# Feeding one expert tile instead of two by choosing products, and requesting gate rows and third down weights later

## What is computed

```python
g_w, g_idx = lax.top_k(g_prob, 1)
...
e_val, e_idx = lax.top_k(e_in, TOP_K)          # two experts of the chosen group
e_w = jax.nn.softmax(e_val, axis=-1) * g_w
...
hid = jax.nn.silu(jnp.einsum('nd,edf->nef', xt, w_gate)) * jnp.einsum('nd,edf->nef', xt, w_up)
hid = hid * combine[:, :, None].astype(hid.dtype)
out = jnp.einsum('nef,efd->nd', hid, w_down)
```

## Time and profile before

| | us |
|---|---|
| median of three runs | 1282.0 |
| lowest, highest | 1281.82, 1284.33 |
| the profiled execution's own time | 1282.83 |
| its span | 1281.0 |
| TensorE busy in the span | 1212.7 (95%) |
| VectorE, ScalarE, POOL busy | 590.9, 441.2, 58.0 |
| share of TensorE in the chain that ended last | 74% |
| share of DMA in that chain | 7% |
| mean granted TensorE clock | 0.991 |

### The profile page before, as it was taken

How to read it: one execution, slowest core, us unless ns; L and a number is a source line. 1 busy time by engine, 2 the same in 40 slices (tenths; PEclk the granted TensorE clock), 3 DMA queues, 4 the chain that set the end, 5 groups by cost and what they waited for, 6 DMA issues and landing times.

```text
span 1281.0 us, 16366 instructions
## 1 busy us (share of the span) xinstructions
PE 1212.7 (95%) x5099; PEld 653.0 (51%) x5100; DVE 590.9 (46%) x1348; ACT 441.2 (34%) x903; POOL 58.0 (5%) x63
## 2 busy tenths in 40 slices
PE   6999999999999999999969998899999999999997
PEld 4555555555554474443325444566654574444443
DVE  1332555555543664222328545887834653222216
ACT  2433656565641121110112326677722111111122
POOL 0103000000000120000021000000000210000002
PEclk9999999999999999999989999899999999999999
DMA  9979999632363177999975001500020369989947
GB/s 370 413 304 376 395 414 413 259 103 103 125 244 144 48 280 232 353 356 360 372 284 224 9 1 50 218 1 2 1 99 1 115 264 331 354 291 333 355 183 266
DMA packets 88641, 289.68 MB, mean 226 GB/s; under 512 B 9369, under 2 KB 27740, under 8 KB 87292
## 3 DMA queue, kind: packets, MB, share of 16 engines
q1 hardware_dynamic: 46176, 185.23, 39.6%
q0 software_dynamic: 16640, 64.59, 13.0%
q10 hardware_dynamic: 25756, 38.98, 9.0%
HBM read 214.03 MB, written 74.73 MB: 225 GB/s over the span
## 4 chain that ended last, share of the span: by engine, by line
PE 74%; DMA 7%; ACT 6%; DVE 5%; SPq 3%; issue 3%; ACTq 1%; DVEq 1%; POOL 0%; POOLq 0%
PE ps L2208 15%; PE ps L1785 11%; PE ps L1804 11%; PE ps L1727 7%; PE ps L2237 6%; PE ps L2088 4%; DMA arena<-in_moe_gu 4%; PE ps L1909 3%; PE ps L2287 3%; PE ps L2051 3%; PE ps L1838 2%; PE ps L2150 2%; ACT arena L746 2%; PE ps L2061 2%; PE ps L1747 2%
## 5 line engine op out<-in xcount | busy, mean ns | idle before, releaser
L2208 PE MATMUL ps<-arena 128*128 (+1 forms) x560 | 246.3, 593 | 0.0
L1727 PE MATMUL ps<-const,arena 128*128 128x128 f32 (+2 forms) x1000 | 145.0, 278 | 24.8 <-DMA const<-in_const 8.1
L2208 PEld LDWEIGHTS ps<-arena 128*128 128x128 f32 x560 | 103.8, 190 | 117.3 <-issue 117.2
L1727 PEld LDWEIGHTS ps<-const,arena 128*128 128x128 f32 (+2 forms) x1000 | 114.8, 142 | 84.9 <-issue 44.5
L1785 PE MATMUL ps<-arena 128*128 128x512 f32 (+2 forms) x400 | 152.1, 535 | 4.8 <-DVE arena L1306 1.4
L1187 DVE TENSOR_REDUCE hst<-ps 128x1 f32<-128x640 f32 (+1 forms) x160 | 111.0, 715 | 85.7 <-PE ps L2088 71.1
L1804 PE MATMUL ps<-arena 128*128 128x512 f32 x320 | 142.0, 597 | 1.4 <-issue 1.4
L2237 PE MATMUL ps<-arena 128*128 (+1 forms) x280 | 126.1, 593 | 2.2 <-ACT arena L890 2.2
L746 ACT ACTIVATE arena<-ps,hst 128x640 f32<-128x640 f32 (+1 forms) x160 | 112.6, 707 | 40.2 <-DVE hst L1187 39.9
L1785 PEld LDWEIGHTS ps<-arena 128*128 128x128 f32 x400 | 74.4, 190 | 74.3 <-issue 58.6
L1804 PEld LDWEIGHTS ps<-arena 128*128 128x128 f32 x320 | 59.1, 190 | 69.8 <-issue 69.7
(11 more groups left out here) (233 smaller groups left out, 1199.7 us busy)
## 6 DMA issues: line engine op xcount, KB each, us to landing
arena<-in_moe_gu SPq DMA_DIRECT2D x128, 512.0 KB, 12.7
arena<-in_ada_w SPq DMA_DIRECT2D x62, 768.0 KB, 11.9
slot_rows<-arena POOLq DMA_DIRECT2D x10, 4096.0 KB, 68.3
arena<-in_moe_w_down SPq DMA_DIRECT2D x64, 512.0 KB, 15.5
slot_rows<-arena ACTq DMA_DIRECT2D x33, 512.0 KB, 9.6
arena<-slot_rows ACTq DMA_DIRECT2D x124, 128.0 KB, 13.6
arena<-mod_rows SPq DMA_DIRECT2D x12, 512.0 KB, 13.2
arena<-in_gqa_w_qkv SPq DMA_DIRECT2D x12, 512.0 KB, 13.7
```

The costliest lines, as they stand in the source:

```text
L1727: return nc.tensor.transpose(out, in_, ident[0:rows, 0:rows])
L2208: last = mm(bank(gu_bank(u)), e_xsT[:, nth(u, D)][:, k * P:(k + 1) * P], w(k * BANK, BANK), start=k == 0, stop=k == KD - 1)
```

## The change

`FED` becomes 1: only tile 0 is made by choosing products, with 128 moving columns instead of 256, in banks 4 and 5. Tile 1 is read back like tile 2, right before it, and transposed on VectorE. What used to hang on the same number but does not change (POOL's list of landings, the counts in the plan) gets a constant of its own, `HELD` = 2. One comparison replaces two in `choose_first`; since tile 0 holds expert 0, it looks at the lower of a token's two row numbers (`R_LOW`), which `place_rows` now keeps. VectorE starts the plan before the copy of the fed tile and no longer has `hid` of tile 0 in its middle; the sums of pair weights move to the end of the layer. TensorE's order for the first two tiles becomes gate/up 0, turn 0, down 0, gate/up 1. SP requests the third down weights after tile 2's rows have landed, and the gate rows and the fetch of modulation vectors in the loop over experts, at expert 4.

```diff
--- before.py
+++ after.py
@@ -113,6 +113,7 @@
...
 GATHERS_EARLY = 3
+GATES_AT = 4
 
@@ -122,7 +123,7 @@
...
 C_R4 = C_CQ + TOK
-FED, FIXED = 2, 3
+FED, HELD, FIXED = 1, 2, 3
 PIECE = 1024
@@ -178,7 +179,8 @@
...
 R_PL = R_BEF + NTILE * NE
-R_FREE = R_PL + 2 * NTILE
+R_LOW = R_PL + 2 * NTILE
+R_FREE = R_LOW + NTILE
 RWC = 32
@@ -562,12 +564,8 @@
...
             load_dn(l, 1)
+            sp.wait_ge(S("xs_landed2", l), 16 * XQ)
             load_dn(l, 2)
-            if l == 0:
-                mod_fetch(1, 1)
-            sp.wait_ge(S("h_ready"), NTILE * (l + 1))
-            for v in range(2):
-                sp.dma_start(gate_m[:, v * D:(v + 1) * D], modrow[l][v, 5:6, :].broadcast_to([P, D])).then_inc(S("gates_m"), 16)
             sp.wait_ge(S("routed"), l + 1)
@@ -577,6 +575,12 @@
...
                     load_dn(l, e + RING_N - 1)
+                if e == GATES_AT:
+                    sp.wait_ge(S("h_ready"), NTILE * (l + 1))
+                    for v in range(2):
+                        sp.dma_start(gate_m[:, v * D:(v + 1) * D], modrow[l][v, 5:6, :].broadcast_to([P, D])).then_inc(S("gates_m"), 16)
+                    if l == 0:
+                        mod_fetch(1, 1)
             end = end_of(NE - RING_N - 1)
@@ -662,15 +666,15 @@
...
 
-            wait_landed(pool, ("gu", l, FED))
+            wait_landed(pool, ("gu", l, HELD))
             pool.nop().then_inc(S("gu_ready"), 1)
-            for e in range(FED, NE):
-                if FED < e < NE - 1:
+            for e in range(HELD, NE):
+                if HELD < e < NE - 1:
                     wait_landed(pool, ("gu", l, e + 1))
...
                 pool.nop().then_inc(S("dn_ready"), 1)
-                if e == FED:
+                if e == HELD:
                     wait_landed(pool, ("gu", l, e + 1))
@@ -904,14 +908,13 @@
...
             act.wait_ge(S("second_fed"), l + 1)
-            for x in range(FED):
-                act.activation(split(e_xsT[:, nth(x, D)][:, BANK:D], KD // 2), split(ps[:, 6 * BANK:8 * BANK], KD // 2)[:, :, x * P:(x + 1) * P],
-                               ACT.Copy).then_inc(S("first_half"), 1)
+            act.activation(e_xsT[:, BANK:D], bank(5), ACT.Copy).then_inc(S("first_half"), 1)
+            act.drain().then_inc(S("y_out", l), 1)
             act.wait_ge(S("rows_scattered"), 32 * NTILE * l + 16 * 2 * NTILE)
-            act.drain().then_inc(S("y_out", l), 1)
             for b in range(RING_N):
                 act.drain().then_inc(S(f"y_stored{b}", l), 16)
-            load_rows(act, l, FED * CAP, FED)
+            for e in range(FED, FIXED):
+                load_rows(act, l, e * CAP, e)
             sil(0, 0)
@@ -1469,16 +1472,17 @@
...
             settle()
+            nc.vector.tensor_tensor(rt(R_LOW + t, 1), pl[:, 0:1], pl[:, 1:2], ALU.min)
             nc.vector.tensor_tensor(slot_i[:, 2 * t:2 * t + 1], pl[:, 0:1], pl[:, 1:2], ALU.min)
...
 
-            oh, rows = e_first[t], const[:, C_IO:C_IO + FED * P]
-            op(nc.vector.tensor_scalar(oh, rows, rt(R_PL + 2 * t, 1), None, ALU.is_equal))
-            op(nc.vector.scalar_tensor_tensor(oh, rows, rt(R_PL + 2 * t + 1, 1), oh, ALU.is_equal, ALU.add)).then_inc(S("first_chosen"), 1)
-
-        def routing(l, first_result):
+            settle()
+            nc.vector.tensor_scalar(e_first[t], const[:, C_IO:C_IO + FED * P], rt(R_LOW + t, 1), None, ALU.is_equal)\
+                .then_inc(S("first_chosen"), 1)
+
+        def routing(l, feed):
 
@@ -1490,7 +1494,7 @@
...
             count, third, slot, big, half = new(TT), new(TT * (NE // RING_N)), new(TT), new(TT), new(TT)
-            need, den = new(ROUNDS), new(T5)
+            need = new(ROUNDS)
             assert n[0] <= 1024, n[0]
@@ -1503,6 +1507,7 @@
...
                 src = dst
+            feed()
             index = const[:, C_TT:C_TT + TT]
@@ -1516,7 +1521,6 @@
...
             op(nc.vector.tensor_reduce(s_row, split(moved, TT), AX.X, ALU.add))
-            first_result()
             nc.vector.tensor_reduce(slot, split(third, TT), AX.X, ALU.add)
@@ -1526,7 +1530,7 @@
...
             nc.vector.scalar_tensor_tensor(s_dn, big, float(RING + 25088 - SLOT - HALF_SLOT * 2), s_dn, ALU.mult, ALU.add)
-            nc.vector.tensor_scalar(s_of, count, float(FED + 1), float((NE - FED) * l - FED), ALU.max, ALU.add)
+            nc.vector.tensor_scalar(s_of, count, float(HELD + 1), float((NE - HELD) * l - HELD), ALU.max, ALU.add)
             nc.vector.tensor_tensor(s_end, c2, const[:, C_GE:C_GE + NE], ALU.add)
@@ -1534,7 +1538,11 @@
...
             nc.vector.tensor_copy(plan[:], stage).then_inc(S("routed"), 1)
-
+            settle()
+
+        def pair_weights(l):
+
+            T5, den = NTILE, rt(T_END, NTILE)
             ex = rt(R_EX, T5 * (NG + 1))
@@ -1602,7 +1610,8 @@
...
             def xsT(t, u, r=0):
-                dve.wait_ge(S(f"xs_landed{u % RING_N}", l), r * 16 * XQ + 16 * XQ)
+                again = FED < u and u % RING_N == FED
+                dve.wait_ge(S(f"xs_landed{u % RING_N}", l), r * 16 * XQ + 16 * XQ * (1 + again))
                 if not isinstance(t, int):
@@ -1619,28 +1628,33 @@
...
 
-            dve.wait_ge(S("first_fed"), l + 1)
-            for x in range(FED):
-                nc.vector.tensor_copy(split(e_xsT[:, nth(x, D)][:, 0:BANK], KD // 2),
-                                      split(ps[:, 4 * BANK:6 * BANK], KD // 2)[:, :, x * P:(x + 1) * P]).then_inc(S("xsT_ready", l), 1)
+            def first_tile():
+                dve.wait_ge(S("first_fed"), l + 1)
+                nc.vector.tensor_copy(e_xsT[:, 0:BANK], bank(4)).then_inc(S("xsT_ready", l), 1)
+
             dve.wait_ge(S("counted"), l + 1)
-            routing(l, lambda: hid(0, 0))
+            routing(l, first_tile)
+            hid(0, 0)
+            hidT(0, 0)
+            xsT(1, 1)
             R = rounds_needed(dve, l)
...
                     for u in range(RING_N):
-                        hidT(i * RING_N + u, u)
                         xsT(i * RING_N + (u + 2), u + 2, i)
                         hid(i * RING_N + (u + 1), u + 1)
+                        hidT(i * RING_N + (u + 1), u + 1)
             for k in range(SLOT_TILES - LOOPED):
-                if l == 0 and k == 1:
-                    modulation(1, 1)
-                hidT(R * RING_N + k, k)
                 if k + 2 < SLOT_TILES - LOOPED:
...
                     hid(R * RING_N + (k + 1), k + 1)
+                if l == 0 and k == 0:
+                    modulation(1, 1)
+                if k + 1 < SLOT_TILES - LOOPED:
+                    hidT(R * RING_N + (k + 1), k + 1)
                 if k == 0:
+                    pair_weights(l)
                     order_weights()
@@ -2143,7 +2157,7 @@
...
                 if t == 0:
-                    pe.wait_ge(S("mix_out"), NTILE * l + LAT + half)
+                    pe.wait_ge(S("mix_out"), NTILE * l + LAT)
                 pe.wait_ge(S("first_chosen"), NTILE * l + t + 1)
@@ -2191,16 +2205,14 @@
...
             def needed(t):
-                return pe.value_load(weights_of[0:1, ds(t, 1)], min_val=1, max_val=2 * (NE - FED))
-
-            def gate_up(t, u, w, ahead, between=None):
+                return pe.value_load(weights_of[0:1, ds(t, 1)], min_val=1, max_val=2 * (NE - HELD))
+
+            def gate_up(t, u, w, ahead):
                 pe.wait_ge(S("xsT_ready", l), t + 1)
...
                     if ahead is None and k == KD // 2:
-                        pe.wait_ge(S("first_half"), FED * l + 1)
-                        if between:
-                            between()
+                        pe.wait_ge(S("first_half"), l + 1)
                     if ahead is not None and k == 2:
@@ -2246,9 +2258,9 @@
...
             gate_up(0, 0, static(("gu", l, 0)), None)
-            pe.wait_ge(S("first_half"), FED * (l + 1))
-            gate_up(1, 1, static(("gu", l, 1)), None, lambda: turn_hid(0, 0))
+            turn_hid(0, 0)
             down(0, 0, static(("dn", l, 0)))
+            gate_up(1, 1, static(("gu", l, 1)), None)
             wait_landed(pe, ("dn", l, 1))
@@ -2361,7 +2373,7 @@
...
         c[:, C_T2 + 4 * FIXED * l:C_T2 + 4 * FIXED * (l + 1)] = (0, CAP, 2 * CAP, 2 * SLOT, 3 * SLOT, 0, SLOT, SLOT + HALF_SLOT, RING + 25088) + \
-            ((NE - FED) * l + 1,) * FIXED
+            ((NE - HELD) * l + 1,) * FIXED
     for x in range(FED):
...
     return c, np.tile(q[ROPE:], (4, 1))
```

## The result

The changed kernel takes 1291.2 us (median of 8 runs, 1288.2 to 1293.7); the kernel before, with its runs of the same occasions, 1283.05. The ratio of the two is put at 1.0053, 95% interval 1.0041 to 1.0066: **slower by 6.8 us (5.3 to 8.5)**; the two medians by themselves lie 8.2 us apart. 1286.2 had been forecast, with a range up to 1289. The profiled execution of the changed kernel took 1289.6.

What follows compares the result with a forecast made beforehand. Layer 1 was taken as bound by TensorE's chain, layer 0 also by bytes still to be moved. 2.4 us (layer 0) plus 1.8 (layer 1) made 4.2 later than the 1282.0 median: 1286.2, range 1280.5 to 1289.

Steps and rivals of the forecast that it cites:

- The choosing products: Last 32 before gate/up: paced by stepped weight loads, so halving moving columns gains 0 us, at most 4.5 a layer.
- Rival 1: Choosing products paced by columns, so gate/up starts sooner and the kernel is faster, 1278 to 1280.5; chance 0.12.
- VectorE before them: Shorter selection ahead of the choosing products; TensorE gains only its idle time, 0.57 us in layer 0, 0.80 in layer 1.
- The new order: First two tiles on TensorE: 20.3 us from gate/up 0 to tile 1's turn, 1.4 and 1.8 us later by layer.
- The transfers: SP's moved requests and later reloads: layer 0 ends 2.4 us later, layer 1's slack hides all of it.
- late second reload: Second gate/up reload in layer 0 needs gate/up of tile 1, so DMA saturates from 502.6, 7.6 us later.
- what DMA had done by then: First reload, third down weights and tile 3's rows moved before saturation; with gate rows set against them, 4.4 us less.
- I take 2.4, between the two: Layer 0's delay, chosen between 3.2 us if paced by bytes and 1.4 if by TensorE's chain.
- the byte branch: Layer 0 paced by bytes still to be moved: 7.6 - 4.4, so it ends 3.2 us later.
- Waits on landed weights in layer 0 longer by 1 to 2 us in sum: Sign to look for: TensorE's waits for gate/up weights, 6.3 us in sum before, grow by 1 to 2.
- DMA near rest between the first and the second reload: Sign to look for: DMA almost idle between the two first gate/up reloads, the second of which goes out later.
- The wait for tile 2's rows: SP waits before the third down weights; the first reload behind still starts at about 491 to 492, against 493.82.

Runs made afterwards that it cites:

- e6: e3 with contiguous columns of hidden rows as the choosing products' weights instead of every eighth (tile 0's columns in another order); one execution, 1291.1 us.
- e3: Changed kernel with all of SP's transfers back at their old places, leaving one fed tile and the new tile order; 1287.5 us, ratio 1.0039.
- e9: Kernel before with only the gate rows moved to expert 4; 1287.1 us, ratio 1.0024.
- e1: Changed kernel with gate rows and modulation fetch requested at their old place again, ahead of the third down weights; 1286.2 us, ratio 1.0028.
- e5: e3 with choosing products 256 columns wide again; 1289.2 us, ratio 1.0042.

## Why the prediction was off

**The choosing products**: right. "They are slower than their columns: the load paces them, and it isn't touched." e6 shows it. By the rule of the Trainium skill (TensorE: Matmul & The Clock Gate, LDWEIGHTS), a load's time goes by its columns alone; 334 against 218 ns for 128 columns in either case speaks against it. The Trainium skill (SBUF — State Buffer, Door 1, note on cachelines) has each access that crosses to a new line of 16 bytes pay a penalty, and with that the trace agrees. Rival 1 was wrong twice: its faster products would have ended in ScalarE's queue (4.51 us idle in e6).

**VectorE before them**: gain of 0.57 and 0.80 us forecast; from the first choosing product to the first gate/up it was 24.98 (457.72 to 482.70) and 25.30 us (1019.71 to 1045.01) before and is 23.90 and 23.85, so 1.1 and 1.4. The earlier choosing products pass a little sooner too (8 in 2.06 us instead of 2.17).

**The new order**: right, 20.44 for 20.3. Layer 1 is 1.2 us longer for 1.8 forecast, by the gain above.

**The transfers**: bytes as the pace of layer 0 was right, the size and the shape were off. Its sum had the late second reload (+7.6), what DMA had done by then (-7.4) and the gate rows (+3.0). The first two cancel, as e3 shows (layer 0 202.4 and 202.6 against 203.1), and the gate rows cost 3.1 us of waits or some more in e9. The step that failed is "I take 2.4, between the two": the byte branch alone was 3.2, and its waits did not spread but stood ahead of one tile, and behind it the clock was at its lower level, 2.2 us more that no term held (2.2 to 2.6 in the four traces; one of the three of the kernel before has 1.7). Layer 0 came out 4.9 us longer: by the means of the traces 1.1 up to the turn of tile 1, 2.3 in waits and 1.8 by the clock, which come to 5.2. "Waits on landed weights in layer 0 longer by 1 to 2 us in sum" (they are 2.4) missed their shape. "DMA near rest between the first and the second reload" was wrong as well: with the down weights and the rows of tiles 3 and 4 beside the first reload DMA is full from 494 on, and until 500 at 269 to 284 GB/s and not at 355. The row at 492.10 holds both reloads, the second of which SP could request only when gate/up 1 was done.

**The wait for tile 2's rows** was taken as free, since the first reload would still leave earlier. It leaves at 492.1, 1.7 us sooner than before but 2.8 us later than it could (489.3, the end of gate/up 0). e1 against e3 puts that at 1.3 us of layer 0, less than the traces of one kernel differ by, so this price stays open.

**Sum**: 4.9 + 1.2 = 6.1 us for 4.2 forecast, inside the measured interval of 5.3 to 8.5. The time lies 5.0 us over the forecast and 2.2 over its range. Of the 5.0, 2.5 are layer 0, 1.7 the end stage in the mean of four executions, for which the prediction had no term, and 1.0 the median of the kernel before, 1283.05 on this occasion and 1282.0 in the prediction; layer 1 takes 0.6 off.

## What to carry to other kernels

Ask of a request that is moved whether it goes from a stretch where DMA is busy but nobody waits into one where every byte is waited for. Here 1 MB cost its 3 us there in full, although nobody needed it before the end of the layer. Price a wait with its shape: the single waits of 5.9 to 8.7 us cost another 2.2 to 2.6 us of slow clock behind them each time, while most waits of 1 to 2 us left the clock at its upper level (two of 2 us did not, for 1.7 us). Profile a kernel more than once: the end stage moved by 5 us between traces of one kernel. And take a change apart before it is judged: a part of it that helps, a plan that is finished 5 us sooner, makes the old kernel 0.3% faster.

## What the runs showed of the hardware

Under weight loads that fill their lane, TensorE's granted clock was at its lower level (1.2 of 2.4 GHz) for parts of these stretches in the kernels with 128 moving columns (0.58 in 470 to 473), and at 1.00 in e5 with 256, at the same number of instructions. The pace did not follow the clock: the 24 products from 467.67 on took 6.07 us, and 6.08 in the kernel before at a clock of 1.00. So products that are paced by a stepped weight load did not pay for the lower clock. e6's contiguous ones did: 24 took 2.94 us at a clock of 1.00, and 32 took 5.46 at a mean clock of 0.72 where that pace makes 3.9.
